# Three rotating PSUM banks for the accumulator halves, and attention steps behind successive units

## The reference, cut to what matters

```python
h    = rms_norm(x, norm_mix_pre)
proj = h @ w_in                       # 2048 x 15664: A q/k/v, B q, B kv + gates, C q/k/v, merge gates
o_a  = dilated_attention(...)         # 8 heads, 3 dilation groups that share one softmax total
o_b  = nsa_attention(...)             # 16 heads: compressed blocks, selected blocks, window
o_c  = diff_attention(...)            # 8 heads, softmax1 - lambda * softmax2, then a norm per head
g    = sigmoid(merge gates)           # 3 x 2048 channels
mix  = g0 * (o_a @ w_branch_a) + g1 * (o_b @ w_branch_b) + g2 * (o_c @ w_branch_c)
x    = x + rms_norm(mix @ w_out, norm_mix_post)
x    = x + rms_norm(relu(rms_norm(x, norm_mlp_pre) @ w_up) ** 2 @ w_down, norm_mlp_post)
```

## Time and profile before

| | us |
|---|---|
| median of 3 runs | 1770.3 (1768.73 to 1770.68) |
| the profiled execution | 1770.19 |
| its span, first to last instruction | 1768.9 |
| TensorE busy (matmuls) | 1722.0 (97%) |
| TensorE weight loads | 1401.1 (79%) |
| VectorE busy | 951.5 (54%) |
| ScalarE busy | 841.3 (48%) |
| GpSimd busy | 55.2 (3%) |
| moved by DMA | 336.77 MB, 190 GB/s over the span |

### The profile page before, as it was taken

The page is one execution under the profiler, slowest core; times in us unless marked ns, Lnnn a source line. Parts: engine busy times, 40 slices in busy tenths (PEclk is TensorE's granted clock), DMA queues, the critical chain, the costliest instruction groups (busy, mean ns, idle before and its releaser), DMA issues.

```text
span 1768.9 us, 23930 instructions
## 1 busy us (share of the span) xinstructions
PE 1722.0 (97%) x8155; PEld 1401.1 (79%) x8155; DVE 951.5 (54%) x1338; ACT 841.3 (48%) x1269; POOL 55.2 (3%) x103
## 2 busy tenths in 40 slices
PE   7999999999999989999999989999999999999998
PEld 6888877777777878787888768888888888888886
DVE  5544455755555544465665465555444455554555
ACT  5443445655555555344444455444443344444442
POOL 1000010000000001000000000000000000000000
PEclk9999999999999999999999999999999999999999
DMA  7666665655566767846876565665556666655553
GB/s 236 204 181 183 194 171 133 171 154 158 164 167 191 183 176 225 277 144 220 291 239 225 190 181 176 190 182 186 190 192 194 195 189 183 188 183 185 193 195 136
DMA packets 168278, 336.77 MB, mean 190 GB/s; under 512 B 11408, under 2 KB 13664, under 8 KB 167680
## 3 DMA queue, kind: packets, MB, share of 16 engines
q1 hardware_dynamic: 162512, 317.17, 58.3%
q0 software_dynamic: 5552, 18.44, 4.5%
q10 hardware_dynamic: 128, 0.03, 0.0%
HBM read 327.11 MB, written 8.49 MB: 190 GB/s over the span
## 4 chain that ended last, share of the span: by engine, by line
PE 57%; DVE 2%; DMA 1%; ACT 1%; issue 1%; SPq 0%; ACTq 0%; DVEq 0%
PE ps L507 18%; PE ps L509 18%; PE ps L508 18%; PE ps L553 1%; DVE w_lo L1325 1%; DMA raw<-in_w_in_dram 1%; DMA gate_dram<-stage 0%; ACT w_hi L933 0%; DVE mid L1975 0%; PE ps L538 0%; PE ps L536 0%; PE ps L537 0%; DVE h_lo L1851 0%; PE ps L723 0%; PE ps L755 0%
## 5 line engine op out<-in xcount | busy, mean ns | idle before, releaser
L1325 DVE TENSOR_TENSOR w_lo<-raw,w_hi 128x1024 fp32r<-128x1024 f32 x576 | 703.2, 1225 | 685.7 <-ACT w_hi L933 666.1
L933 ACT ACTIVATE w_hi<-raw 128x1024 fp32r<-128x1024 f32 x576 | 607.2, 1059 | 636.1 <-PE ps L509 614.5
L507 PE MATMUL ps<-w_hi,h_hi 128*128 128x512 f32 (+1 forms) x1600 | 635.1, 397 | 21.7 <-ACT stage L1062 11.5
L509 PE MATMUL ps<-w_hi,h_lo 128*128 128x512 f32 (+1 forms) x1600 | 623.7, 390 | 0.0
L508 PE MATMUL ps<-w_lo,h_hi 128*128 128x512 f32 (+1 forms) x1600 | 623.0, 389 | 0.0
L507 PEld LDWEIGHTS ps<-w_hi,h_hi 128*128 128x128 f32 x1600 | 302.0, 189 | 104.2 <-issue 29.9
L509 PEld LDWEIGHTS ps<-w_hi,h_lo 128*128 128x128 f32 x1600 | 301.9, 189 | 63.5
L508 PEld LDWEIGHTS ps<-w_lo,h_hi 128*128 128x128 f32 x1600 | 302.5, 189 | 58.7
L507 PE MATMUL ps<-w_hi,u_hi 128*128 128x512 f32 x496 | 193.4, 390 | 0.0
L508 PE MATMUL ps<-w_lo,u_hi 128*128 128x512 f32 x496 | 193.0, 389 | 0.0
L509 PE MATMUL ps<-w_hi,u_lo 128*128 128x512 f32 x496 | 193.0, 389 | 0.0
(11 more groups left out here) (270 smaller groups left out, 925.8 us busy)
## 6 DMA issues: line engine op xcount, KB each, us to landing
raw<-in_w_in_dram SPq DMA_DIRECT2D x240, 512.0 KB, 3.7
raw<-in_w_up_dram SPq DMA_DIRECT2D x128, 512.0 KB, 3.8
raw<-in_w_down_dram SPq DMA_DIRECT2D x128, 512.0 KB, 4.3
raw<-in_w_out_dram SPq DMA_DIRECT2D x32, 512.0 KB, 4.2
bias<-bias_table POOLq DMA_DIRECT2D x72, 128.0 KB, 3.5
raw<-in_w_branch_b_dram SPq DMA_DIRECT2D x16, 512.0 KB, 5.5
raw<-in_w_branch_c_dram SPq DMA_DIRECT2D x16, 512.0 KB, 5.1
gate_dram<-stage SPq DMA_DIRECT2D x12, 512.0 KB, 5.8
```

The lines of the kernel that those rows point to most:

```text
L507: pe.matmul(acc, hi[:, kc + k, tok], w_hi[:, slot, k, 0:cols], start=a, stop=False)
L509: mm = pe.matmul(acc, lo[:, kc + k, tok], w_hi[:, slot, k, 0:cols], start=False, stop=b)
L933: act.activation(w_hi[:, slot, :, :], raw[:, slot, :, :], ACT.Copy).then_inc(sem("hi_ready"), 1)
L1325: dve.tensor_tensor(w_lo[:, slot, :, :], raw[:, slot, :, :], w_hi[:, slot, :, :].bitcast(F32), ALU.subtract).then_inc(sem("lo_ready"), 1)
```

## The change

Five things change, all in the attention stretch.

1. The halves of a chunk c gather in bank `SLOT_BANKS[(2c + t) % 3]`, t being the half: chunk 0 in banks 0 and 1, chunk 1 in 6 and 0, chunk 2 in 1 and 6, and again. All evictions read from there.
2. TensorE's order of halves is new for the first two and the last two units of a chunk: half 0 of both, then half 1 of the first with the steps of its slot, then half 1 of the second with its steps. Half 0 of a new chunk waits for the copy of half 1 of the chunk before the last, half 1 for the copy of half 0 of the last chunk.
3. Outputs go to bank 7 alone.
4. The slots of pairs: branch A t = s + 7 (before 9), o = s + 8 (10); branch B t = s + 3 (3), o = s + 4 (6); branch C t = s + 4 (5), o = s + 5 (10). Stage tiles of slots 12, 21 and 30 go to 10, 19 and 28.
5. The norm of branch C moves four slots up. Its transposes go to slots 152 to 155 (before 152, 153, 155, 157) and to banks 7 and 5, their splits one and two slots up; the compressed probabilities are transposed into banks 4 and 5 (before 6 and 7).

```diff
-            pairs.append(Pair("a", 9 * k + g, 9 * k + 9 + g, 9 * k + 10 + g, 4 * g + k, 4 * g + k, 8 * g + 2 * k, 1,
+            pairs.append(Pair("a", 9 * k + g, 9 * k + 7 + g, 9 * k + 8 + g, 4 * g + k, 4 * g + k, 8 * g + 2 * k, 1,
...
-        pairs.append(Pair("b", 38 + 3 * q, 41 + 3 * q, 44 + 3 * q, h, h // 4 + 2 * br, 24 + 2 * h, 1,
+        pairs.append(Pair("b", 38 + 3 * q, 41 + 3 * q, 42 + 3 * q, h, h // 4 + 2 * br, 24 + 2 * h, 1,
...
-        pairs.append(Pair("c", 89 + 5 * h, 94 + 5 * h, 99 + 5 * h, h, h, 40 + h, 0, 12 + h, True, True))
+        pairs.append(Pair("c", 89 + 5 * h, 93 + 5 * h, 94 + 5 * h, h, h, 40 + h, 0, 12 + h, True, True))
...
-STAGE_T = {12: 6, 21: 7, 30: 8, 33: 9, 42: 10, 49: 11, 57: 12, 66: 13}
+STAGE_T = {10: 6, 19: 7, 28: 8, 33: 9, 42: 10, 49: 11, 57: 12, 66: 13}
...
-C_AT = [2, 3, 5, 7]
-SPLIT_AT = [2, 2, 3, 4, 6, 8, 16, 16, 17, 17]
+C_AT = [2, 3, 4, 5]
+C_BANKS = [7, 5]
+SPLIT_AT = [2, 2, 3, 4, 5, 6, 16, 16, 17, 17]
+
+
+SLOT_BANKS = [0, 1, 6]
+O_BANK = 7
+
+
+def slot_bank(c, t):
+    return SLOT_BANKS[(2 * c + t) % 3]
...
+        def taken(c, t):
+
+            if c < 10:
+                return ("evac_s", S0["q_b"] + c + 1) if t else ("evac_v", V0["q_b"] + c + 1)
+            return "evac_s", S0["gate"] + 2 * (c - 10) + 1 + t
+
+        def slot_half(n, t):
+
+            c, s = divmod(n, CH)
+            cols = B_LAST if c == 3 else W
+            pe.wait_ge(sem("lo_ready"), XS + n + 1)
+            if s == 0:
+                if c == 0:
+                    pe.wait_ge(sem(("evac_v", "evac_s")[t]), (V0, S0)[t]["q_b"])
+                elif t:
+                    name, value = taken(c - 1, 0)
+                    pe.wait_ge(sem(name), value)
+                elif c == 1:
+                    pe.wait_ge(sem("tevac_v"), 6)
+                    pe.wait_ge(sem("tevac_s"), 6)
+                else:
+                    name, value = taken(c - 2, 1)
+                    pe.wait_ge(sem(name), value)
+            acc, tok, slot = ps[:, slot_bank(c, t), 0:cols], slice(t * P, (t + 1) * P), n % RING
...
+            if t:
+                mm.then_inc(sem("unit_used"), 1)
+            elif s == CH - 1:
+                mm.then_inc(sem("half_done"), 1)
...
-            bank = 6 + pr.out % 2
+            bank = O_BANK
             pe.wait_ge(sem("pt_copied1"), p + 1)
             if pr.first:
-                wait(pe, sem("o_taken"), pr.out - 1)
+                wait(pe, sem("o_taken"), pr.out)
...
-            c, s = divmod(n, CH)
-            unit(Pos(XS + n), s % RING, h_hi, h_lo, UR * s, 0, B_LAST if c == 3 else W, s == 0, s == CH - 1,
-                 slot_free(c) if s == 0 else None)
+            s = n % CH
+            if s in (0, CH - 2):
+                slot_half(n, 0)
+                slot_half(n + 1, 0)
+            elif s not in (1, CH - 1):
+                slot_half(n, 0)
+            slot_half(n, 1)
...
-            act.activation(stage[:, 0, h, :], ps[:, h, :], ACT.Tanh, scale=rstd_half[:, h:h + 1]).then_inc(
+            act.activation(stage[:, 0, h, :], ps[:, slot_bank(c + 10, h), :], ACT.Tanh, scale=rstd_half[:, h:h + 1]).then_inc(
...
-        act_steps = {33: [bgate_tanh], 137: [c_root_step], B0 + 5: [gelu_tanh], B0 + 10: [cmp_exp]}
+        act_steps = {33: [bgate_tanh], 133: [c_root_step], B0 + 5: [gelu_tanh], B0 + 10: [cmp_exp]}
```

More of the change, by code:

```diff
@@ L629, in _ @@
             values("v_a", i)
[L630 to L634, removed]
+        def taken(c, t):
[19 more added lines that the diff above has]
+            acc, tok, slot = ps[:, slot_bank(c, t), 0:cols], slice(t * P, (t + 1) * P), n % RING
+            for k in range(UR):
+                kc = UR * s + k
+                pe.matmul(acc, h_hi[:, kc, tok], w_hi[:, slot, k, 0:cols], start=kc == 0, stop=False)
+                pe.matmul(acc, h_hi[:, kc, tok], w_lo[:, slot, k, 0:cols], start=False, stop=False)
+                mm = pe.matmul(acc, h_lo[:, kc, tok], w_hi[:, slot, k, 0:cols], start=False, stop=kc == KC - 1)
+            if t:
+                mm.then_inc(sem("unit_used"), 1)
+            elif s == CH - 1:
+                mm.then_inc(sem("half_done"), 1)
         def late_tiles(n):
@@ L750, in cmp_scores @@
             pe.wait_ge(sem("compressed"), 1)
-            pe.wait_ge(sem("pt_copied1"), NPAIR)
+            pe.wait_ge(sem("o_split_lo"), 6)
             for t in range(2):
@@ L764, in cmp_transposes @@
                 q, t = n // 2, n % 2
-                tr = pe.transpose(ps[:, 6 + n // 4, P * (n % 4):P * (n % 4) + P],
+                tr = pe.transpose(ps[:, 4 + n // 4, P * (n % 4):P * (n % 4) + P],
                                   cmp_p[:, t, 4 * q:4 * q + 4, :].rearrange("p a n -> p (a n)"), ident[:, :])
@@ L780, in output_transposes @@
             pe.wait_ge(sem("c_ready"), 1)
+            pe.wait_ge(sem("pt_copied1"), NPAIR)
             pe.wait_ge(sem("o_taken"), 20)
@@ L1044, in evacuate @@
             dst = v_c[:, 1, W * (c - 8):W * (c - 7)] if c >= 8 else stage[:, c % 2, 1, 0:cols]
-            act.activation(dst, ps[:, 1, 0:cols], ACT.Copy, scale=scale).then_inc(sem("evac_s"), 1)
+            act.activation(dst, ps[:, slot_bank(c, 1), 0:cols], ACT.Copy, scale=scale).then_inc(sem("evac_s"), 1)
         def late_out(n):
@@ L1104, in take @@
             act.wait_ge(sem("pv_done"), p + 1)
-            src = ps[:, 6 + pr.out % 2, 0:256]
+            src = ps[:, O_BANK, 0:256]
             if pr.kind == "a":
@@ L1116, in take @@
                 for t in range(2):
-                    sq = act.activation(c_square[:, t, :], ps[:, 6 + pr.out % 2, P * t:P * t + P], ACT.Square,
+                    sq = act.activation(c_square[:, t, :], ps[:, O_BANK, P * t:P * t + P], ACT.Square,
                                         accum_out=c_ssq[:, t, h:h + 1])
@@ L1469, in evacuate @@
             dst = v_c[:, 0, W * (c - 8):W * (c - 7)] if c >= 8 else stage[:, c % 2, 0, 0:cols]
-            dve.tensor_scalar(dst, ps[:, 0, 0:cols], scale, None, ALU.mult).then_inc(sem("evac_v"), 1)
+            dve.tensor_scalar(dst, ps[:, slot_bank(c, 0), 0:cols], scale, None, ALU.mult).then_inc(sem("evac_v"), 1)
         def late_out(n):
@@ L1692, in cmp_third @@
             dve.wait_ge(sem("cmp_pt"), 1)
-            dve.tensor_copy(cmp_pt[:, :, :].rearrange("p (b a) n -> p b (a n)", b=2), ps[:, 6:8, :]).then_inc(
+            dve.tensor_copy(cmp_pt[:, :, :].rearrange("p (b a) n -> p b (a n)", b=2), ps[:, 4:6, :]).then_inc(
                 sem("cmp_pt_copied"), 1)
```

8 lines of the change are left out of this document (4 added, 4 removed).

## The result

The changed kernel takes 1764.79 us (median of 9 runs, 1759.92 to 1766.89) beside 1770.3 (9 runs, 1768.73 to 1775.85): ratio 0.9963, 95% interval [0.9951, 0.9975]. It is faster, by 5.5 us where 13.3 were forecast, and it lies just outside the range.

What follows compares the result with a forecast made beforehand. The prediction took TensorE, busy 97% of the span, as the bound. From the profiled 1770.2 us it removed 25.4 and added 12.0, giving 1756.8, forecast as 1757 us, range 1750 to 1764.

Steps and rivals of the forecast that it cites:

- the copy is due 8.85 us after unit 23 ends, against 7.9: Branch A transposes near VectorE's head copies: the copy ends in time, so the `p_t` wait of 1.0 us goes.
- With the waits go the two slow stretches, 3.4 us: Behind the waits at 247.5 and 573.3: TensorE's two stretches at 1.2 GHz vanish with the boundary waits, 3.4 us removed.
- Boundaries, 21.0 of waits: Chunk starts in the attention stretch: all 12 waits for an emptied bank go, 18.1 us plus 12 x 0.24.
- `dup`, +1.0: Key tiles of unit 33: TensorE's wait for VectorE's copies grows from 1.0 to 2.0 us.
- Separate groups, 3.2: Attention steps on TensorE: outputs no longer followed by scores in 16 groups, each paying 0.20 for edges, 3.2 us added.
- Branch C, 2.7: Transposes four units behind scores: waits of 1.6 and 0.4 at units 94 and 104, with edges and 0.2, add 2.7 us.
- The tanh of chunk 11, 0.2: Within the branch C forecast: this tanh is due at 5.8 and ends at 6.0, adding 0.2 us.
- Gate store, 4.3: At the compression weights: gate chunk 5's store lands after 15.1 us, chunk 6's tanh is 4.0 late, 4.3 with edge.
- A: Rival at the compression weights: the gate store lands in time; without 4.3 and 0.8 the kernel takes 1752; chance 0.22.
- B: Rival: weight burst delays the store 3 us more, slow stretches follow there and in branch C; 1762; chance 0.18.
- C: Rival: boundary waits move instead of going, the gate chunks' 11.5 us returning as waits for `w_lo`; 1769; chance 0.07.
- D: Rival: each branch C chain is 3 us longer than counted, waits 18.2 in place of 2.0; 1773; chance 0.06.

Runs made afterwards that it cites:

- first profile: The profiled execution among the nine runs of the whole changed kernel; it took 1759.92 us, the lowest of the nine.
- A alone: Three banks and new order of halves, with only branch A's steps and its tile groups at new places, against the kernel before: 1756.15 us, ratio 0.992.
- the head-copy variant: The whole changed kernel with VectorE's first head copies moved from behind unit 24 to behind unit 26: 1761.84 us, ratio 0.9952 to the kernel before.
- the spread weights: The whole changed kernel with the eight compression weight loads each behind a further unit, not in one burst: 1758.85 us, ratio 0.9942 to the kernel before.
- second profile: The profiled execution when the whole changed kernel was run again unedited: it took 1765.11 us; median of those runs 1764.28, ratio 0.9964.
- B alone: Three banks and new order of halves, with only branch B's steps at new places, against the kernel before: 1753.39 us, ratio 0.9909.
- candidate 1: Three banks, new order, old step places; head copies behind unit 28, `dup` tile behind 34, weight loads spread over 8 units: 1744.51 us, ratio 0.9855.

## Why the prediction was wrong

The direction and the mechanism of the gain were right; two steps failed. The first is a distance priced too long, the second the slow stretches of TensorE's clock.

**First, "the copy is due 8.85 us after unit 23 ends, against 7.9".** It was due at 6.8 and ended at 9.9. Unit 23 ended at 305.92 and TensorE could have begun the second transposes at 315.93 - 3.21 = 312.72. My 8.85 is three units of 2.72 and the transposes before. But units 24 to 31 have 304 columns: their matmuls follow each other at 0.138 (306.05 - 305.92 and on) and such a unit takes 12 x 0.138 = 1.66. Three are 5.0, not 8.2 (this is the step that failed), and with the 0.84 + 0.2 behind `scale` and 0.6 of transposes this is the 6.8. The 9.9 has the eight head copies (1.43), `v_b` and a whole split between the first transposes' end and the copy. The prediction gives no working for its 7.9, so which entry of VectorE's queue it had too short stays open. So in place of the 1.0 that was to go, 3.0 came (4.05 against 1.04), with one edge more and 1.4 of transposes and outputs at the lower clock. A `w_lo` wait of 0.95 follows; it stands only in the kernels with A's new places. That TensorE runs through the narrow units faster than the splits is my reading of it and isn't tested. This term was booked at -1.0 and measures about +5.8 = 3.0 + 0.24 + 1.4 + 0.95 + 0.24; -1.0 to +5.8 is 6.8 of error. That the head copies are part of it is shown (moving them took 1.5), and that branch A's places bring the waits is shown from both sides.

**Second, "With the waits go the two slow stretches, 3.4 us".** Those two went, and so did a third at 781 us (7 matmuls), which the prediction hadn't counted. But two new ones came with the longer waits for `p_t` and `dup`. After, first profile:

```profile
315.00:320.00 5.00, 4.07 (x22) 3.06 (x23) 3.89 (x7) 1.44 (x2) 0.00 (x0) 0.66 0.62 168
340.00:345.00 5.00, 2.15 (x11) 1.77 (x10) 4.16 (x13) 2.25 (x4) 0.00 (x0) 0.78 0.68 204
345.00:350.00 5.00, 5.00 (x24) 4.15 (x24) 3.54 (x9) 3.25 (x8) 0.00 (x0) 0.88 0.37 109
```

The granted clock (0.66, 0.78, 0.88) falls short of 1 by 0.34, 0.22 and 0.12, and 5 us x their sum is 3.4 us, 0.002 of the span. That is also how far the median clocks lie apart: 0.996 to 0.998 in the kernels with three banks and branch A's old places, 0.994 to 0.996 in the four with A's new places (the kernel after, A alone, the head-copy variant, the spread weights). The stretch at 315 stands in every profile with A's new places but that of the moved head copies, and in none with the old ones.

The second profile has three stretches more (4.4), and most runs are like it: a median clock of 0.994 to 0.995. No profile ties these three to the steps. They stand behind the wait for the gate tanh, at 777 us and at 1040 us. The kernel before has one at 781 too, and the kernel with banks and order alone has one at 1023. Whether they come isn't fixed by the trace of one execution, and why one wait of 2.0 is followed by the lower clock and one of 2.3 isn't stays open.

The other terms:

- *Boundaries, 21.0 of waits*: right. Eleven are gone in every kernel with three banks and the order of halves. The twelfth, at the compression weights, is booked under the gate store below. With the steps left in place the whole part comes to 21.5 us by the medians, 20.2 by the ratio.
- *`dup`, +1.0*: measured +1.8. The reason I gave (groups moved ahead) isn't the main one: the wait is 2.91 with the steps at their old places too. In the trace before a boundary wait stood just ahead of it,

```profile
336.35 0.47 PE L507 MATMUL ps<-w_hi,h_hi 128*128 128x512 f32 x1 [1.56 <-DVE stage L1470]
```

  and 1.02 of the earlier trace rows + 1.56 + 0.24 is 2.82: by this sum the removed wait came back one step later. The steps alone fit it from the other side: there the boundary wait is 2.83 and none for `dup` is left.
- *Separate groups, 3.2*: right. 23 groups more and 5.6 us, of which 1.4 and 0.9 are small matmuls at the lower clock; the rest is 3.3. B alone: 13 groups, 2.9.
- *Branch C, 2.7*: right, at the places named (timeline of TensorE, behind units 98 and 108):

```profile
581.26 0.52 PE L723 MATMUL ps<-ident,logits 128*128 128x128 f32 x3 [1.39 <-DVE logits L1632]
...
613.34 0.52 PE L723 MATMUL ps<-ident,logits 128*128 128x128 f32 x3 [0.47 <-DVE logits L1632]
```

  1.86 + 0.48 = 2.3 with edges. The tanh of chunk 11, 0.2, was in time.
- *Gate store, 4.3*: the mechanism right, the size off. The store was issued 5.7 after the start of the weights (686.16 - 680.44), as counted, and landed after 13.2 and not 15.1, so the wait was 2.3. The Trainium skill ("DMA: Bandwidth & Descriptors", section "Queues, rings and completion order") has the engines take turns between queues, from which the prediction estimated a landing some 12 us after the weights began, at 692.4; it landed at 699.3. By that estimate there would have been no wait, and there was one, so the estimate falls; how the packets were shared wasn't looked at.
- *Left over*: matmuls outside groups and waits took 2.1 us less in the stretch than before (some 1.4 to 3.1 in the kernels with three banks). I didn't trace it. It is what remains of the stretch when the rest is taken off, so the sum below closes by construction.

For the first profile the sum is then 1770.2 - 21.0 - 3.8 (three slow stretches before, less the few large matmuls behind `dup`) + 5.8 + 1.8 + 0.9 + 3.3 + 2.3 + 2.5 - 2.1 = 1759.9 (0.9 is the `dup` tile group at the lower clock), as measured. This lies inside the stated range only because errors of both signs met: the 6.8 of the first step against 2.6 too much for the gate store with its slow stretch and the 2.1 left over. The 4.4 of lower clock, as in the second profile, brings it near the median.

Of the rivals, A had it right that the store lands sooner than forecast, and B that slow stretches follow the waits. B's 1762 is the nearest time, by luck: its store was to land 3 us later than forecast and landed 2 sooner. C and D didn't happen. That the moved steps would take back most of the gain was in no rival, since I priced their places by a sum of small edges.

## What to carry to other kernels

Price cover in time, not in units, and look at the width of each unit that stands in the distance: three narrow units made a distance of 8.2 us one of 5.0. When a wait is taken out, add it to the next wait on the same path before calling it gone. Time a change of two parts in two halves: here one brought 21 us and the other cost 15.

## What was not expected of the hardware

- The same wait in two executions of one kernel (2.30 and 1.99 us) was followed by TensorE at 2.4 GHz in one and by 8 matmuls at 1.2 GHz in the other (pitch 0.23 and 0.43). With two more such stretches this made 4.4 of the 5.2 us between the two executions. Nine runs of the kernel spread over 7 us, with mean clocks of 0.996 to 0.994.
- A DMA write of 0.52 MB took 13.2 us to land within a burst of eight loads of 0.52 MB on another queue, and at most 7.6 with the same loads each behind a further unit. In candidate 1, with the same spacing at another place, one still took 9.95.
